# A two-layer hybrid encoder in fp32 on one core: reordering the query norm, its rotation and the convolution taps inside the attention stage

## The reference

```
x += 0.5 * swiglu(rms_norm(x), ffn1)
h = rms_norm(x);  p = h @ w_in          # columns: RWKV | conv | attention | gates
y_rw  = rwkv7 (two directions, 8 heads of 64)
y_cv  = depthwise conv, 31 taps over time, 512 channels, layer norm, silu, @ w
y_mla = latent attention, 8 heads: q, k = rms_norm over (64 plain + 32 rotary) values per head,
        rotary turned by position, softmax(q k) v, @ w
x += (sigmoid(gates) * (y_rw, y_cv, y_mla)) summed over the three @ w_o
x += 0.5 * swiglu(rms_norm(x), ffn2)
```

## Time and profile before

| | us |
|---|---|
| median of three runs (1632.86 to 1642.88) | 1642.8 |
| the profiled execution, its own time | 1646.6 |
| its span (first to last instruction) | 1644.7 |
| TensorE busy in it | 1560.4 (95%) |
| VectorE busy | 1174.0 (71%) |
| ScalarE busy | 760.6 (46%) |
| granted TensorE clock, mean | 0.982 |

### The profile page before, as it was taken

One profiled execution on the slowest core, in us unless ns is written; L12 is line 12 of the kernel. 1 busy time (PEld: TensorE's weight loads), 2 busy tenths in 40 slices (PEclk: granted clock), 3 DMA queues, 4 the chain that ended last, 5 costly groups with the idle time before them and its releaser, 6 DMA issues.

```text
span 1644.7 us, 40178 instructions
## 1 busy us (share of the span) xinstructions
PE 1560.4 (95%) x17083; PEld 1444.8 (88%) x17083; DVE 1174.0 (71%) x1739; ACT 760.6 (46%) x1169; POOL 90.1 (5%) x103
## 2 busy tenths in 40 slices
PE   6999999998898999999999999999989989999999
PEld 6999897777788899999899999868788888999998
DVE  4777776787886576777666766769887765777764
ACT  5444564465161345444444445545721613554442
POOL 1000120000030001000100001200000300010000
PEclk9999999899999999999999999989998999999999
DMA  5855542232011345655556555323320213566554
GB/s 179 274 181 182 190 141 90 78 116 78 17 61 47 104 154 169 194 185 185 191 197 230 185 187 179 116 65 116 103 67 16 73 35 103 156 182 193 187 183 153
DMA packets 61940, 227.92 MB, mean 139 GB/s; under 512 B 6896, under 2 KB 7920, under 8 KB 60880
## 3 DMA queue, kind: packets, MB, share of 16 engines
q1 hardware_dynamic: 60624, 218.26, 41.1%
q0 software_dynamic: 1152, 7.21, 1.2%
HBM read 224.69 MB, written 1.05 MB: 137 GB/s over the span
## 4 chain that ended last, share of the span: by engine, by line
PE 76%; DVE 13%; ACT 5%; issue 3%; DMA 2%; ACTq 0%; SPq 0%; DVEq 0%; POOLq 0%
PE banks L568 16%; PE banks L570 15%; PE banks L569 15%; PE banks L634 10%; PE banks L635 5%; DVE wlo L1516 3%; PE banks L979 2%; DVE cvx L1766 2%; DMA raw<-in_stream 2%; ACT whi L1139 2%; DVE arena L1993 1%; PE banks L860 1%; ACT arena L1334 1%; PE banks L746 1%; PE banks L991 1%
## 5 line engine op out<-in xcount | busy, mean ns | idle before, releaser
L1516 DVE TENSOR_TENSOR wlo<-raw,whi 128x1024 fp32r<-128x1024 f32 x411 | 506.4, 1235 | 298.9 <-ACT whi L1139 297.6
L1139 ACT CAST whi<-raw 128x1024 fp32r<-128x1024 f32 x411 | 429.4, 1048 | 465.4 <-PE banks L570 318.9
L568 PE MATMUL banks<-hx,whi 128*128 128x256 f32 x1696 | 487.0, 287 | 21.3 <-DVE wlo L1516 17.4
L569 PE MATMUL banks<-hx,whi 128*128 128x256 f32 x1696 | 481.3, 284 | 0.0
L570 PE MATMUL banks<-hx,wlo 128*128 128x256 f32 x1696 | 481.2, 284 | 0.0
L568 PEld LDWEIGHTS banks<-hx,whi 128*128 128x128 f32 x1696 | 326.7, 193 | 28.3 <-DVE wlo L1516 16.8
L569 PEld LDWEIGHTS banks<-hx,whi 128*128 128x128 f32 x1696 | 326.9, 193 | 0.2
L570 PEld LDWEIGHTS banks<-hx,wlo 128*128 128x128 f32 x1696 | 326.8, 193 | 0.0
L634 PE MATMUL banks<-gg,whi 128*128 128x512 f32 x704 | 244.3, 390 | 0.0
L568 PE MATMUL banks<-h,whi 128*128 128x256 f32 x760 | 230.5, 303 | 9.9 <-ACT arena L1237 5.4
L569 PE MATMUL banks<-h,whi 128*128 128x256 f32 x760 | 219.4, 289 | 0.0
(11 more groups left out here) (298 smaller groups left out, 1912.5 us busy)
## 6 DMA issues: line engine op xcount, KB each, us to landing
raw<-in_stream SPq DMA_DIRECT2D x411, 512.0 KB, 3.5
arena<-in_wuq POOLq DMA_DIRECT2D x2, 1152.0 KB, 11.7
lo_w<-in_lora POOLq DMA_DIRECT2D x2, 1024.0 KB, 7.9
arena<-in_wukv POOLq DMA_DIRECT2D x2, 1024.0 KB, 14.9
xT<-in_x SPq DMA_DIRECT2D x1, 1024.0 KB, 4.9
out<-xT SPq DMA_DIRECT2D x8, 128.0 KB, 3.4
consts<-in_cst SPq DMA_DIRECT2D x1, 642.5 KB, 8.4
masks<-in_msk POOLq DMA_DIRECT2D x1, 288.0 KB, 4.0
```

The lines of the kernel that those rows point to most:

```text
L568: TE.matmul(o, wh, hi, start=first, stop=False, **kw)
L569: TE.matmul(o, wh, lo, start=False, stop=False, **kw)
L1139: SE.copy(whi[:, m % HL, :], raw[:, m % RAW, :]).then_inc(hi_ready, 1)
L1516: TT(wlo[:, m % HL, :], raw[:, m % RAW, :], whi[:, m % HL, :].bitcast(F), ALU.subtract)\
```

## The change

- TensorE: the spreads for the plain queries stand ahead of the turning and of its wait, no longer behind it.
- VectorE: `q rotary normed` stands directly behind `inverse`, ahead of the low part, the gate product and the four taps; the four taps stand behind `q normed`.
- The point `scored` (20 pieces) is split into `scored first` (2) and `scored` (18). With 2 pieces one more column tile is complete; ScalarE and VectorE do their share for it ahead of `exps(0)` and `pair_probs(0)`.
- Taps: the two per RWKV tile are gone; 10 more stand in front of the wait for `k turned`, 13 new ones behind `k rotated`; in the pair loop six and four per pair instead of four; one less per level of the inverse. Of 124 taps 27 are left for the RWKV part (15 in its levels, 12 behind them), where there were 44 and 42 (20 in the levels).

```
-FILL_A1 = {... "turned": 12, "scored": 20}
+FILL_A1 = {... "turned": 12, "scored first": 2,
+           "scored": 18}
...
 (TensorE)
-                pe.wait_ge(*vec.at("q rotary normed"))
-                m = TE.matmul(bank[1][:, :], cc("rot", P), qr[:, :, :], start=True, stop=True)
-                m.then_inc(*ten.mark("q turned"))
                 pe.wait_ge(*act.at(("v", 1)))
                 for j in range(PAIRS):
                     m = spread(bank[2 - 2 * (j // 2)][:, (j % 2) * S:(j % 2 + 1) * S], SUMS, HD, (2 * j, 2 * j + 1))
                     if j % 2:
                         m.then_inc(*ten.mark(("q spread", j // 2)))
+                pe.wait_ge(*vec.at("q rotary normed"))
+                m = TE.matmul(bank[1][:, :], cc("rot", P), qr[:, :, :], start=True, stop=True)
+                m.then_inc(*ten.mark("q turned"))
                 fa.at("turned")
...
                 scores(0)
+                fa.at("scored first")
                 fa.at("scored")
...
 (ScalarE)
+                fa.at("scored first")
                 exps(0)
                 fa.at("scored")
...
 (VectorE)
-                        if n >= T.RW:
-                            conv(2)
                         yield
...
-                conv(16)
+                conv(26)
                 ve.wait_ge(*ten.at("k turned"))
...
                 TT(kr0, kr0, krt, ALU.add).then_inc(*vec.mark("k rotated"))
+                conv(13)
                 fa.at("squares")
                 conv(8)
                 ve.wait_ge(*act.at("rms"))
                 V.reciprocal(rn8[0:2 * SUMS, 0, :], rn8[0:2 * SUMS, 0, :]).then_inc(*vec.mark("inverse"))
-                fa.at("inverse")
-                conv(4)
                 pairs = lambda b: bank[b].rearrange("p (j t) -> p j t", j=2)
                 ve.wait_ge(*ten.at("q rotary spread"))
                 STT(qr, qr, vv("qk_q_r"), pairs(1), ALU.mult, ALU.mult).then_inc(*vec.mark("q rotary normed"))
+                fa.at("inverse")
                 ve.wait_ge(*ten.at("k rotary spread"))
...
                         ALU.mult, ALU.mult).then_inc(*vec.mark(("q normed", g)))
+                conv(4)
                 fa.at("turned")
...
+                pair_max(0)
+                fa.at("scored first")
                 conv(6)
-                pair_max(0)
                 pair_probs(0)
                 fa.at("scored")
                 for p in range(PAIRS):
                     if p + 1 < PAIRS:
                         pair_max(p + 1)
-                    conv(4)
+                    conv(6)
                     fa.at(("pair", p))
                     if p + 1 < PAIRS:
                         pair_probs(p + 1)
+                    conv(4)
                     fa.at(("turned pair", p))
...
                         if d == 0:
-                            conv(4)
+                            conv(3)
```

More of the change, by code:

```diff
@@ L194 @@
 PAIRS = RC
-FILL_A1 = {"latent squares": 12, "latents normed": 24, "squares": 20, "inverse": 10, "turned": 12, "scored": 20}
+FILL_A1 = {"latent squares": 12, "latents normed": 24, "squares": 20, "inverse": 10, "turned": 12, "scored first": 2,
+           "scored": 18}
 for _p in range(PAIRS):
```

5 lines of the change are left out of this document (1 added, 4 removed).

## The result

| | before | changed |
|---|---|---|
| median of four runs, us | 1642.84 (1632.86 to 1643.98) | 1616.21 (1609.06 to 1619.51) |
| ratio, 95% interval | | 0.9858 [0.9819, 0.9896] |
| profiled execution, us | 1646.6 | 1617.59 |
| span; TensorE busy; the difference, its idle time | 1644.7; 1560.4; 84.3 | 1615.8; 1546.5; 69.3 |
| mean granted clock | 0.982 | 0.988 |

26.6 us faster in the medians; the ratio, which is not that of the medians, makes it 23. Of the 28.9 us by which the profiled span shrank, 15.0 are idle time of TensorE and 13.9 its busy time, though it does the same 17083 matmuls. Of these 13.9 the clock accounts for 10.2: the stretches at 0.50 add up to 58.0 us before and 37.5 after, and half of the difference is 10.2. For the other 3.7 there is no row (the ends of matmuls are modelled in this profile).

The account below looks back on a forecast made before the run. TensorE, busy 95% of the span, was taken as the bound, leaving its waits and half-clock time to win. 3.0 + 4.8 - 0.6 + 6.8 + 3.2 + 1.2 + 2.0 = 20.4 us off 1642.8 gave 1622 us, range 1616 to 1628.

Parts of the forecast that it names:

- the new wait: TensorE waiting for the third column tile's copy, behind the exponentials: 0.3 us lost per layer, 0.6 in all.
- First wait: TensorE's 1.5 us wait for VectorE before the turning goes in each layer: gain 3.0 us.
- Fits by 0.8: Normed queries for scores(0) ready at 288.6, TensorE supplied with other work until 289.4: no late wait there.
- Second wait: TensorE's waits of 2.6 and 2.2 us for ScalarE's copy of the second RWKV tile go: gain 4.8 us.
- Clock: Attention stage: half-clock stretches at the turning shrink from 10.24 to 3.41 us, gain 6.8; those behind the column wait go, 3.2.
- Loop: Fewer VectorE taps between the normed queries and the pair loop's end; half their saving counted, gain 1.2 us.
- Levels: One tap less between VectorE's two steps of each RWKV level: 1.0 us per layer, gain 2.0 us.
- Early waits: Taps added before `k turned` (ten) and behind `k rotated` (thirteen) fill VectorE's idle time and cost nothing.
- half is given back in the loop: Rival: VectorE paces the pair loop, TensorE's early arrival becomes longer waits, half the sum remains: 1632.5 us; chance 0.11.
- The clock never falls: Rival: with the wait before the turning gone, no slow stretch remains there; another 3.4 us, 1619; chance 0.22.
- The slower rival: Taps ahead of the tile rounds make low parts late in the pair loop, adding waits and slow stretches: 1653 us; chance 0.04.

Follow-up runs that it names:

- e5: The changed kernel itself, unaltered, run once more beside three variants on one chip; median 1612.81 us, ratio 0.9851 to the kernel before.
- e3: Kernel before plus only the first-tile part: two pieces of `scored` ahead of the first exponentials, maximum ahead of the first taps; ratio 0.9998.
- e12: Changed kernel with the redistribution of the taps undone; ratio 0.9926 to the kernel before.
- e1: Kernel before plus only TensorE's new order, query spreads ahead of the turning; ratio 0.9936.
- e2: Kernel before plus only VectorE's early rotary norm, ahead of low part, gate product and taps; ratio 0.9961.
- e6: Changed kernel with TensorE's turning put back between the spreads, VectorE's early norm kept; ratio 0.9882 to the kernel before.
- e4: Kernel before plus only the redistribution of VectorE's taps; ratio 0.9915.
- e9: Changed kernel with four taps instead of three in each RWKV level of the first direction; median 1613.75 us, ratio 0.9859 to the kernel before.
- e10: Changed kernel with one tap instead of three in each RWKV level, the rest behind the levels; median 1612.68 us, ratio 0.9839 to the kernel before.
- e11: Changed kernel with every maximum of the loop ahead of the low part of the column tile before it; 1612.23 us, ratio 0.9846 to the kernel before.
- e7: Changed kernel with the first-tile part undone on all three engines; ratio 0.9874 to the kernel before.

## Why the prediction was right

The forecast was 1622.0; 1616.2 and, in e5, 1612.8 were measured. The forecast's own range is 1616 to 1628: the first lies at its lower end, the second below it. That range does not follow from the bounds that it names: with the loop at 4.9 or -3, the levels at 3.2 or 0 and the new wait at 0 or 1.5 per layer the sum goes from 1617 to 1631, and the clock's bounds are not in it. By its steps:

- **First wait, 3.0:** right. The turning has no wait, and scores(0) begins at 288.90 without one; "Fits by 0.8" held, with the normed queries there at 287.1.
- **Second wait, 4.8 less 0.6:** the wait went, but the step "the exponentials themselves start later by one tile round, but the probabilities are needed only after scores(1) and eight more pieces" failed. The third tile's copy is on time; what is late is the second maximum, and 1.40 per layer stand at the first product instead of 0.3 at a column tile. e3 and e12 show the same wait at 3.77 and 3.78 where the taps are not moved.
- **Clock, 6.8 + 3.2:** in the first pair of profiles exactly that, 10.24 to 3.41 twice and 3.41 to nothing twice; in e5's runs the whole clock, that of other stages with it, gives 8.9 ± 8.2. The reason given for the short stretch (only the turning and column tiles behind the spreads) is borne out by e1 and e2 and by the 26 stretches under e6. The order of the change has 6.83 in the first layer of half of its eight profiles, so the 3.4 that remain are rather 4.
- **Loop, 1.2: mis-sized.** This is the term that failed: the taps took 3.6 us from the products' waits (4.9 to 1.3 in e4), three times what was put on them. VectorE's 91% in the loop was read as half of its saving arriving. That it had fallen behind by the loop's first pair was not seen, and there the taps ahead of the second maximum count in full: 2.4 us of them in e12, and 2.4 us of wait.
- **Levels, 2.0:** 1.2 by the waits of all profiles, 1.7 by e9's alone.
- **Early waits, nothing:** right; no wait of TensorE between 255 us and the loop.

There is luck in the sum. The loop's term was 2.4 too small, and the new wait, 2.8 instead of 0.6, was 2.2 too small as well; the two misses cancel.

Of the rivals, "half is given back in the loop" is what happens without the taps (e3, e12): the profile's 91% was evidence for it, and this change contains its own remedy. "The clock never falls" came only in two second layers of the eight profiles with the change's order (e10, e11). The Trainium skill (TensorE: Matmul & The Clock Gate, "What's actually happening") has activity lift the half clock. The trace agrees where column tiles run, at 285.75, and not behind the spreads, where TensorE was busy for all 3.41 us from 282.34 at 0.50, with no wait ahead. The slower rival did not occur: no low part is waited for.

The measured gain (26.6 and 24.3) is 4 to 6 us above the 20.4. In the attention stage 9.7 us of waits went where the terms have 8.4: at the products 1.3 net (3.6 by the taps, less what the late maximum costs) instead of 0.6, and a second, smaller column wait of 0.6. Outside it 5.3 us of idle time went, some 2 of them in the levels. The other 3 are mostly waits in the RWKV part that name no releaser; the second profile of the same kernel has 2.6 us more idle time (71.9) than the first, so they may be scatter. This stays open, as does what the early norm adds once the spreads stand first: that variant was not run, and e1's rows leave it, as far as waits go, 0.61 per layer.

## What to carry to other kernels

The worth of a reordering is not a sum over its parts: alone they give 11.9, 5.8, -0.6 and 15.2 us, together 24 to 27, and the part that is worth nothing alone takes 3 us of waits out beside the others, and up to 3.4 of half clock. Where a helper engine is nearly full, look for the instruction that its list makes late for the *next* consumer: a wait that is closed by moving work ahead can come back at the next place which that work now stands in front of. And before pricing a stage from one pair of profiles, undo that one edit: a reading of 3 to 6 us for the levels came down to 1 to 2.

## What was not expected of the hardware

**The spread of this kernel's runs is mostly the clock.** The four first runs of the changed kernel took 1609.06, 1614.83, 1617.59 and 1619.51 us at granted clocks of 0.995, 0.992, 0.988 and 0.987; without the clock's part they are 1601.0, 1601.9, 1598.2 and 1598.5.

**The clock falls at the row of 8-row matmuls, in ten of the profiles with TensorE busy and no wait ahead.** In all 14 profiles with their 28 layers a stretch at 0.50 lies at the spreads and the turning, but for two layers, whether TensorE had waited or not. Its length goes with how long the spreads run on behind the fall: 3.41 us when they are over, 6.83 when they end 0.9 to 2.7 us later, 10.24 when they end 4.4 to 6.6 later.

**The same wait is followed by a stretch at half clock in one kernel and not in the other.** Column tile of before, second layer, and of e4, first layer:

```profile
1109.64 0.39 PE L568 MATMUL banks<-h,whi 128*128 128x256 f32 x1 [2.24 <-ACT arena L1237]
```

```profile
301.05 0.39 PE L568 MATMUL banks<-h,whi 128*128 128x256 f32 x1 [2.24 <-ACT arena L1237]
```

```profile
300.26:303.67 3.41, 2.62 (x22) 2.62 (x23) 3.21 (x5) 3.26 (x8) 0.00 (x0) 1.00 0.00 0
```

Behind the first the clock is 0.50 for 3.41 us, at the second (e4's window, last row) it stays at 1.00. So in this kernel a slow stretch that follows a wait is a risk that goes with it and no fixed price.

**A stretch of 17.07 us** lies behind a short wait without releaser in the second layer's RWKV part in four of the 14 profiles (before, changed, e6, e7), where 1.78, 1.56, 1.00 and 1.54 us were waited; in the other ten that wait was 0.73 to 1.29 and no such stretch followed. So the wait's length does not decide it alone: 1.00 was followed by it in e6, 1.29 was not elsewhere. It costs 8.5 us, as much as a third of this change.
